# A feed-forward block computed as two-by-two block products: gate and up with seven products of block sums in place of eight

## What is computed

```python
D_FF = 2816
def rmsnorm(x, g):
    y = xf * lax.rsqrt(jnp.mean(xf * xf, axis=-1, keepdims=True) + EPS)
    return (y * g.astype(jnp.float32)).astype(x.dtype)
def swiglu(xn, w_gu, w_down):
    g, up = jnp.split(xn @ w_gu, 2, axis=-1)
    return (jax.nn.silu(g) * up) @ w_down
def trunk(...):
    for i in range(DEPTH):                       # DEPTH = 2
        ...                                      # norm, mixer, residual
        x = x + swiglu(rmsnorm(x, g_ffn[i]), f_w_gu[i], f_w_down[i])
    y = rmsnorm(x, g_final)
```

## Time and profile before

| | |
|---|---|
| profiled execution, its own time | 3015.9 us |
| its span from the first to the last instruction | 3014.1 us |
| median of three runs | 3014.09 us |
| PE busy / its weight loads | 2928.4 us (97%) / 2878.2 us (95%) |
| DVE busy | 1610.9 us (53%) |
| POOL busy | 1068.5 us (35%) |
| ACT busy | 408.6 us (14%) |
| mean granted TensorE clock | 0.989 |

### The profile page before, as it was taken

How to read it: one execution, slowest core, us unless ns; L and a number is a source line. 1 busy time by engine, 2 the same in 40 slices (tenths; PEclk the granted TensorE clock), 3 DMA queues, 4 the chain that set the end, 5 groups by cost and what they waited for, 6 DMA issues and landing times.

```text
span 3014.1 us, 41963 instructions
## 1 busy us (share of the span) xinstructions
PE 2928.4 (97%) x16670; PEld 2878.2 (95%) x16670; DVE 1610.9 (53%) x2328; ACT 408.6 (14%) x693; POOL 1068.5 (35%) x452
## 2 busy tenths in 40 slices
PE   6899999999999999999999999999999999999998
PEld 6899989899999999999899999999999999999998
DVE  6465564795555555555833465610655555555555
ACT  4112020230000000000311211200300000000004
POOL 4232223233333333333233223343433333333331
PEclk8999999999999999999999999999999999999999
DMA  2131121211111111111011121111111111111111
GB/s 92 43 70 39 49 44 42 51 36 42 42 42 41 37 40 42 42 42 42 28 43 42 32 68 42 36 42 42 43 42 42 42 42 42 42 42 42 42 42 63
DMA packets 198924, 133.76 MB, mean 44 GB/s; under 512 B 6731, under 2 KB 188619, under 8 KB 198860
## 3 DMA queue, kind: packets, MB, share of 16 engines
q1 hardware_dynamic: 198860, 132.87, 15.4%
HBM read 122.34 MB, written 10.51 MB: 44 GB/s over the span
## 4 chain that ended last, share of the span: by engine, by line
PE 89%; DVE 8%; issue 1%; POOL 1%; ACT 1%; DVEq 0%; POOLq 0%; ACTq 0%
PE ps L638 83%; DVE xn_lo L1353 2%; PE ps L1086 1%; DVE sq_f L1346 1%; POOL w_hi L594 1%; PE ps L1008 1%; PE ps L832 1%; PE ps L888 1%; PE ps L860 0%; PE ps L894 0%; PE ps L890 0%; PE ps L868 0%; PE ps L783 0%; DVE xT L1643 0%; DVE h_hi L1637 0%
## 5 line engine op out<-in xcount | busy, mean ns | idle before, releaser
L638 PE MATMUL ps<-xn_hi,w_hi 128*128 128x384 f32 x3480 | 1190.8, 342 | 16.7 <-DVE xT L1369 8.0
L594 POOL TENSOR_TENSOR w_hi<-w_raw,ones 128x1024 fp32r<-128x1024 f32 x213 | 535.1, 2512 | 1866.9 <-PE ps L638 1850.2
L638 PE MATMUL ps<-xn_lo,w_hi 128*128 128x384 f32 x3480 | 1178.5, 339 | 0.0
L638 PE MATMUL ps<-xn_hi,w_lo 128*128 128x384 f32 x3480 | 1178.2, 339 | 0.0
L638 PEld LDWEIGHTS ps<-xn_hi,w_hi 128*128 128x128 f32 x3480 | 657.6, 189 | 20.7 <-DVE xT L1369 8.2
L638 PEld LDWEIGHTS ps<-xn_lo,w_hi 128*128 128x128 f32 x3480 | 657.6, 189 | 1.5 <-issue 0.6
L638 PEld LDWEIGHTS ps<-xn_hi,w_lo 128*128 128x128 f32 x3480 | 656.9, 189 | 0.0
L598 POOL TENSOR_TENSOR w_lo<-w_raw,w_hi 128x1024 fp32r<-128x1024 f32 x213 | 528.7, 2482 | 16.7
L1685 DVE TENSOR_TENSOR xT<-xT,ps 128x384 f32<-128x384 f32 x528 | 279.5, 550 | 166.1 <-PE ps L638 166.0
L638 PE MATMUL ps<-hg_hi,w_hi 128*128 128x384 f32 x1056 | 358.5, 340 | 0.8 <-DVE xT L1685 0.8
L638 PE MATMUL ps<-hg_hi,w_lo 128*128 128x384 f32 x1056 | 356.5, 338 | 0.0
(11 more groups left out here) (262 smaller groups left out, 2342.3 us busy)
## 6 DMA issues: line engine op xcount, KB each, us to landing
w_raw<-in_f_w_gu_dram SPq DMA_DIRECT2D x88, 512.0 KB, 3.7
w_raw<-in_f_w_down_dram SPq DMA_DIRECT2D x44, 512.0 KB, 3.5
w_raw<-in_b_w_in_dram SPq DMA_DIRECT2D x32, 512.0 KB, 4.0
w_raw<-in_a_w_in_dram SPq DMA_DIRECT2D x24, 512.0 KB, 4.1
w_raw<-in_b_w_out_dram SPq DMA_DIRECT2D x16, 512.0 KB, 3.5
out_dram<-y_out SPq DMA_DIRECT2D x9, 512.0 KB
x_in<-in_x_prompt_dram SPq DMA_DIRECT2D x8, 512.0 KB, 5.7
c_nat<-in_state_C_dram SPq DMA_DIRECT2D x8, 512.0 KB, 5.9
```

Of the source, the lines that this page charges most:

```text
L594: nc.gpsimd.tensor_tensor(w_hi[s][:, :, :], w_raw[r][:, :, :], ones[:, :].unsqueeze(1).to_broadcast([P, KD, P]), ALU.mult)\
L638: ins = pe.matmul(out, w[slot][:, k, :], x(k), start=(first and n == 0), stop=(last_one and n == total - 1))
```

## The change

Gate and up are computed as products of two-by-two block matrices. For one of them, the two units c of 128 output features are the block rows, the two halves of the 1024 contraction features (KH = 4 blocks of 128 each) are the inner index, and two neighbouring quarters of the tokens (QT = 288 tokens) are the block columns; two such pairs s cover the 1152 tokens. Plain, a pair needs eight block products. The changed kernel makes seven (P1 to P7), each of a block or sum of blocks of the weights and a block or sum of blocks of the tokens, and gets the four results by adding products: P1+P2; (P1+P6+P5)+P7; P3+(P1+P6+P5); P4+(P1+P6+P7). One product is 4 contraction blocks x 3 passes = 12 matmuls of 288 columns.

- The sums of token blocks are made once for a layer, while its first iteration runs; they stand as seven blocks for each pair s (`xs_hi`, `xs_lo`). So the first iteration of a layer computes plainly, eight block products for a pair, also with 288 columns (`first_piece`), and ten iterations use the seven.
- The sums of weight blocks are made by POOL for every iteration, four of 128x512 for gate and four for up. Rounding weights (`round_left`) is now ACT's, the rest (`lower`) is POOL's, both in halves of 128x512. A weight half has one of 18 positions in an iteration: 0 to 6 gate, 7 to 13 up, 14 to 17 down; it takes the place of the one six positions ahead in the three slots, so it waits until PE has done with that.
- A product is added to its PSUM bank's neighbours by DVE: ACT copies P1 to SBUF (`keep_p1`, into the not yet used `hg_hi`), DVE adds P6, P5 and P7 in turn, then P2, P3 and P4. The gate result goes to SBUF (`hidden32`), Silu runs there in place, and ACT also rounds the hidden values (`hidden_hi`). All eight PSUM banks hold products now, in the down projection as well.
- The loads of the feed-forward weights wait for the rests of the halves that they overwrite, not for whole units.
- The down projection keeps its 144 matmuls of 384 columns.

```diff
 W_GATES = WeightPhase(None, 1, [0], [5])
 W_HEADS = WeightPhase(W_GATES, H, [2, 1, 0, 2, 0, 2, 1, 0], [3, 3, 3, 3, 2, 2, 5, 3])
...
+P1, P6, P5, P7, P2, P3, P4 = range(7)
+RIGHT = [X_B11, X_T2, X_T1, X_T3, X_B21, X_B22, X_T4]
+BANK_OF = [0, 1, 2, 3, 0, 2, 3]
+STEPS = [(P1, 0), (P1, 1), (P6, 0), (P6, 1), (P5, 0), (P5, 1), (P7, 0), (P7, 1),
+         (P2, 0), (P3, 0), (P4, 0), (P2, 1), (P3, 1), (P4, 1)]
...
+FINALS = [(0, 1), (1, 1), (0, 0), (0, 2), (0, 3), (1, 0), (1, 2), (1, 3)]
+FIRST_GATE = [(0, 0), (1, 0), (0, 1), (1, 1), (0, 2), (0, 3), (1, 2), (1, 3)]
+FIRST_UP = [(0, 1), (1, 1), (0, 3), (1, 3), (0, 0), (0, 2), (1, 0), (1, 2)]
+LAST_GROUP = [0, 1, 2, 2]
...
@@ -602,10 +742,59 @@
...
-            with pool.Fori(0, N_FFN) as i:
-                for u in range(6):
-                    split_unit(W_FFN0, i, u)
...
+                with pool.Fori(0, N_FFN - 1) as i:
+                    for kind in range(2):
+                        def low(j):
+                            lower(i, 7 * kind + j, left_source(j))
...
+                        low(P1)
...
+                        nc.gpsimd.tensor_tensor(left_sum[:, :, :], raw_half(1, 0), raw_half(1, 1), ALU.add)\
+                            .then_inc(left_summed, 1)
+                        pool.wait_ge(left_summed, so_far(1))
+                        nc.gpsimd.tensor_tensor(raw_half(1, 0), raw_half(1, 0), raw_half(0, 0), ALU.subtract)\
...
+                        nc.gpsimd.tensor_tensor(raw_half(0, 0), left_sum[:, :, :], raw_half(0, 0), ALU.subtract)\
+                            .then_inc(left_summed, 1)
+                        low(P6)
...
@@ -940,62 +1127,104 @@
...
+            def ffn(layer, n, bank_free):
...
+                def combine(out, pos, x, s, first, last_one, ready=None):
+                    for k in range(KH):
...
+                        for m, (w, r) in enumerate(((w_hi, xs_hi), (w_hi, xs_lo), (w_lo, xs_hi))):
+                            ins = pe.matmul(out, left(layer, w, pos)[:, k, :], r[:, s, x, k, :],
+                                            start=(first and k == 0 and m == 0),
...
+                        if g == 0:
+                            pe.wait_ge(hl, step(i, 8, 7 if first else 5))
+                        elif g == 1:
+                            pe.wait_ge(hl, step(i, 8, 8))
...
+                for c, q in FIRST_UP:
+                    pe.wait_ge(gs, FIRST_GATE.index((c, q)) + 1)
+                    first_piece(1, c, q)
+                down(0, True)
+                pe.wait_ge(x_los, 40 * (layer + 1))
+                with pe.Fori(0, N_FFN - 1) as i:
+                    for kind in range(2):
+                        for j, s in STEPS:
+                            if s == 0:
+                                pe.wait_ge(left_lo, prepared(layer, i, 7 * kind + j))
+                            o = BANK_OF[j]
+                            if j == P2:
+                                pe.wait_ge(p1_kept, product(layer, i, kind, s))
+                            elif j == P3:
+                                pe.wait_ge(p5_added, product(layer, i, kind, s))
+                            elif j == P4:
+                                pe.wait_ge(p7_added, product(layer, i, kind, s))
+                            elif kind == 0:
+                                pe.wait_ge(da, step(i, N_DOWN, 4 * s + o + 1))
+                            else:
+                                pe.wait_ge(gs, step(i, 8, finished(s, o)))
+                            combine(bank(4 * s + o, QT), 7 * kind + j, RIGHT[j], s, True, True)\
+                                .then_inc(prod_mm[j], 1)
+                    down(i, False)
...
@@ -1254,17 +1484,167 @@
...
-            def ffn(layer):
-                with act.Fori(0, N_FFN) as i:
-                    for c in range(2):
-                        for g in range(NG):
-                            act.wait_ge(g_scaled[layer], i * 6 + 3 * c + g + 1)
-                            act.activation(silu[:, c, g, :], bank(g), ACT.Silu).then_inc(g_silu[layer], 1)
...
+                def body(i, last_one):
+                    keep_p1(i, 0)
+                    round_sum(i, 0, P4, 6, prod_mm[P1], product(layer, i, 0, 1))
+                    for j in range(6):
+                        round_sum(i, 1, j, 7 + j, prod_mm[j + 1], product(layer, i, 0, 1))
+                    for at, (s, o) in enumerate(FINALS):
+                        act.wait_ge(g_scaled[layer], step(i, 8, at + 1))
+                        gated(i, s, o)
+                    keep_p1(i, 1)
+                    round_sum(i, 1, P4, 13, prod_mm[P1], product(layer, i, 1, 1))
+                    for pos in range(14, 17):
+                        round_down(i, pos, prod_mm[pos - 13], product(layer, i, 1, 1))
+                    for at, (s, o) in enumerate(FINALS):
+                        if at == 5:
+                            round_down(i, 17, prod_mm[P2], product(layer, i, 1, 1))
+                        hidden_hi(i, at, s, o)
+                    if not last_one:
+                        round_ahead(i)
...
@@ -1653,47 +2045,174 @@
...
+                for at, (c, q) in enumerate(FIRST_UP[4:], 4):
+                    hidden_lo(0, at - 1, FIRST_UP[at - 1][1] // 2, first_bank(*FIRST_UP[at - 1]) % 4)
+                    dve.wait_ge(first_mm, 16 * layer + 8 + at + 1)
+                    hidden(0, at, q // 2, first_bank(c, q) % 4)
+                hidden_lo(0, 7, FIRST_UP[7][1] // 2, first_bank(*FIRST_UP[7]) % 4)
...
+                        if kind == 1:
+                            for at, (s, o) in enumerate(FINALS):
+                                scale_silu(i, at, at, s, o)
+                        for s in range(2):
+                            dve.wait_ge(prod_mm[P6], product(layer, i, kind, s))
+                            dve.wait_ge(p1_kept, product(layer, i, kind, s))
+                            dve.tensor_tensor(piece_of(hg_hi32, s, 1), piece_of(hg_hi32, s, 0),
+                                              bank(4 * s + 1, QT), ALU.add)\
+                                .then_inc(p6_added, 1)
...
+                        for s in range(2):
+                            dve.wait_ge(prod_mm[P7], product(layer, i, kind, s))
+                            dve.wait_ge(p5_added, product(layer, i, kind, s))
+                            dve.tensor_tensor(piece_of(hg_hi32, s, 3), piece_of(hg_hi32, s, 1),
+                                              bank(4 * s + 3, QT), ALU.add)
+                            dve.tensor_tensor(bank(4 * s + 1, QT), piece_of(hg_hi32, s, 2),
+                                              bank(4 * s + 3, QT), ALU.add)\
+                                .then_inc(p7_added, 1)
+                            dve.wait_ge(p7_added, product(layer, i, kind, s))
+                            finish(s, s, 1)
...
+                            for n_, (j, o) in enumerate(((P2, 0), (P3, 2), (P4, 3))):
+                                at = 2 + 3 * s + n_
+                                dve.wait_ge(prod_mm[j], product(layer, i, kind, s))
+                                dve.tensor_tensor(bank(4 * s + o, QT), bank(4 * s + o, QT), piece_of(hg_hi32, s, o),
+                                                  ALU.add).then_inc(u_added, 1)
+                                dve.wait_ge(u_added, final_sum(layer, i, kind, s, n_))
+                                finish(at, s, o)
+                                if kind == 1 and at > 2:
+                                    hidden_lo(i, at - 1, *FINALS[at - 1])
+                    hidden_lo(i, 7, *FINALS[7])
```

More of the change, by code:

```diff
@@ L451, in _, with ffn @@
                 head(h)
-            def ffn(layer, phase):
+            def ffn(layer, before):
                 gu = f_w_gu[layer].rearrange("(k p) n -> p k n", p=P)
                 down = f_w_down[layer].rearrange("(k p) n -> k p n", p=P)
-                with sp.Fori(0, N_FFN) as i:
-                    for c in range(2):
-                        load(phase, i, 2 * c, gu[:, :, bass.ds(i * (2 * P) + c * P, P)])
-                        load(phase, i, 2 * c + 1, gu[:, :, bass.ds(i * (2 * P) + (D_FF + c * P), P)])
-                    for c in range(2):
-                        load(phase, i, 4 + c, down[bass.ds(i * 2 + c, 1)].rearrange("o p n -> (o p) n"))
@@ L463, in _, with load_gu, load_down @@
-            ffn(0, W_FFN0)
+                def load_gu(i, kind, c):
+                    sp.dma_start(w_raw[c][:, :, :], gu[:, :, bass.ds(step(i, 2 * P, kind * D_FF + c * P), P)])\
+                        .then_inc(f_loaded[c], 16)
+                def load_down(i, c):
+                    sp.dma_start(w_raw[c][:, :, :].rearrange("p k n -> p (k n)"),
+                                 down[bass.ds(step(i, 2, c), 1)].rearrange("o p n -> (o p) n")).then_inc(f_loaded[c], 16)
+                for c in range(2):
+                    sp.wait_ge(split, before.end - c)
+                    load_gu(0, 0, c)
@@ L616, in _ @@
                     split_unit(W_BO, i, u)
```

(9 more changed lines are left out.)

547 lines of the change are left out of this document (423 added, 124 removed).

## The result

The changed kernel took 2910.18 us (median of 4 runs, 2908.28 to 2916.6) against 3016.56 (3012.18 to 3020.6): a ratio of 0.9656, 95% interval 0.9638 to 0.9673. The forecast was 2931, range 2896 to 2992, so the time is inside it and 21 us under its middle. The profiled execution took 2909.89 with a span of 2908.2; before it was 3015.9 and 3014.1. So 106 us went where 83 were forecast.

A forecast was written before the change was run, and what follows sets the result against it. The loop was taken as bound by PE's matmul stream alone. 100.2 saved in the loops, less 3.0 for plain first iterations and 14 for layer starts, gives 83.2: 3015.9 to 2932.7, median 2931 us, range 2896 to 2992.

The forecast's parts named there:

- The stream, 135.6 ns: Gate and up in the loop: 336 matmuls of 288 columns at 135.6 ns, 5.01 us less an iteration, 100.2 in twenty.
- the three readings: Cost of a 288-column matmul: 135.6 ns (excess per instruction), 131.7 (per column) or 175.6 (weight load sets it).
- The down projection keeps its 25.3 us.: Down projection of each loop iteration: 144 matmuls at 175.6 ns, 25.3 us, unchanged.
- The other engines hide: Loop: POOL 32.5, ACT 19, DVE 40.2 us stay under PE's 70.9; fifth rest ready 0.8 us early; cost nothing.
- additions from PSUM are not held: DVE in the loop: the 28 additions of products, each with one PSUM input, do not contend with POOL.
- The layer starts, +14: Start of both layers' parts: waits and clock falls cost 8 us more in layer 1, 6 in layer 0; bounds 0 to 30.
- The 62 operations: DVE at layer 1's start, reciprocals to seventh rest: 62 x 0.45 + 4 x 1.3 = 33 us, so PE waits 5.5.
- T: Time zero for layer 1's start: the end of the mixer's matmuls; the seventh rest was put at T + 63.5.
- A: Rival for the matmul stream: excess belongs to the columns, 131.7 ns, 29 us less, 2902; chance 0.16.
- B: Rival: loop chain late at fifth rest or P5's addition; at 3 us an iteration 60 lost, 2991; chance 0.22.
- C: Rival: weight load sets the pace, 288 columns still cost 175.6 ns, 3231; decides above 146.7 ns; chance 0.09.
- D: Rival: starts of the layers' parts cost 30 or more, 2947 and up; mild form within the forecast's 0.50.

The follow-up runs named there:

- the second trace: The changed kernel run once more, unaltered, beside the two new start orders: 2907.20 us, ratio to before 0.9640.
- The run with eight banks: The kernel before with its down projection over eight PSUM banks in turn instead of six: 2996.27 us, ratio to before 0.9952.
- The new order: Changed kernel with ACT and DVE making token sums T4 behind the hidden values at each layer's start: 2894.13 us; with weight halves rounded earlier too, 2891.17.

## Why the prediction was right, and where it was off

- **The stream, 135.6 ns.** The choice among the three readings was right: an excess of the instruction, 14.4 ns in the loop against 15.6 put. The error was in the 15.6. It was a mean over two paces of the kernel before, 173.33 and 176.67, which I had seen as iterations of 75.1 and 76.4 and averaged. The changed loop has 134.4, and the term for gate and up measured 1010.9 - 903.4 = 107.5 us (20 iterations) instead of 100.2. Against the quick pace of before the products are worth 49.92 - 45.17 = 4.75 us an iteration at 134.4, and 49.92 - 44.80 = 5.12 at the 133.3 of the second trace's layer 0; 5.01 was put. Of the 107.5, 20 x 4.75 = 95 are the products and the other 12.5 are the 13 slow iterations of before, 0.96 us each.
- **"The down projection keeps its 25.3 us."** This step failed: it put the change of banks in the down projection at nothing. It fell to 24.96, and with the short waits that went the loops gave another 9.6 us. Of mixer B's 5.1 us 3.4 are two falls of the clock in the trace of before, as the rows above show. A wait of 90 ns, too small for the table of waits, had cost the kernel before some 18 us, most of them through the pace that it redrew. The run with eight banks shows it: it takes the 18 without any of the seven products. The changed kernel is 2996.3 - 2910.2 = 86 us faster than that one. That this is close to the 83 of the forecast is in part luck: between these two traces the loops give 94.1 (100.2 forecast), the starts take 14.7 (17.0 with the plain iterations), and mixer B gives 8.8, where the run with eight banks had three falls of the clock.
- **The other engines hide.** Right, and tight: the fifth rest is ready 0.65 us early (0.8 forecast) in all twenty iterations, by this row of DVE's timeline against the down projection's start at 967.49; it is held from 965.34 on while POOL works.

```profile
965.34 1.50 DVE L2088 TENSOR_TENSOR hg_lo<-hidden,hg_hi 128x288 fp32r<-128x288 f32 x1
```

```profile
965.24 1.29 POOL L751 TENSOR_TENSOR w_lo<-w_raw,w_hi 128x512 fp32r<-128x512 f32 x1 [5.16 <-ACT w_hi L1492]
```

  That additions from PSUM are not held was read right: the one at 1473.44 in the earlier trace rows ran beside this operation of POOL, the next behind that of the earlier trace rows.

```profile
1473.18 2.61 POOL L598 TENSOR_TENSOR w_lo<-w_raw,w_hi 128x1024 fp32r<-128x1024 f32 x1
```

- **The layer starts, +14.** The sum was right (with the plain iterations 17.0 forecast, 14.9 measured), its parts were not all. The waits: 3.8 for the weights (5.3 forecast), 5.3 and 6.5 at the first down projection (5.5); in layer 0 1.5 for the sum of squares and 1.0 for the first scaled gate, where 3 for token rests and 1.5 were put. The clock: two falls of 1.7 were put for layer 1, but a granted clock of 0.93 over 92.9 us is up to 6.5 us lost instead of 3.4 (up to, because PE waited anyway in a part of it). And the wait at the first down projection came out by luck. The 62 operations in its sum are a miscount: the list (8 + 8 + 24 + 7 + 7) has 54, which makes 29.5 us in place of 33, the seventh rest at T + 59.5 and a wait of 1.5, not 5.5. By its own list the forecast had no wait of that size. The trace has one because DVE was not busy to the end, as I had it: it idles there, behind ACT (DVE's timeline, then ACT's):

```profile
2110.79 7.37 DVE L2064 RECIPROCAL rstd_f<-rstd_f 128x384 f32<-128x384 f32 x3
...
2145.50 0.45 DVE L2083 TENSOR_TENSOR hidden<-hidden,ps 128x288 f32<-128x288 f32 x1
2148.89 0.46 DVE L2088 TENSOR_TENSOR hg_lo<-hidden,hg_hi 128x288 fp32r<-128x288 f32 x1 [2.94 <-ACT hg_hi L1525]
```

```profile
2145.25 3.27 ACT L1514 ACTIVATE xs_hi<-xs_lo 128x1152 fp32r<-128x1152 f32 x3 [0.55 <-DVE xs_lo L2112]
2148.43 0.42 ACT L1525 ACTIVATE hg_hi<-hidden 128x288 fp32r<-128x288 f32 x1
```

  ACT rounds token sums, which nobody needs before the second iteration, while the fifth hidden value waits behind them in its queue. From the reciprocals to the seventh rest DVE worked 29.7 us, as the 54 operations give, and idled for 4.5; eight operations too many in the count stood in for idle times that were not foreseen. The new order removes the wait of both layers.
- **The rivals.** A (excess by the column) gave 2902, nearer to the time than my forecast, and is wrong all the same: 512 columns take 227 ns, not the 231 of a column's share. What spoke for it, the 5 ns over 107 at 128 columns of float32, is no excess but the floor: float32r matmuls of 128 to 224 columns start the same 111.5 ns apart. B's mechanism is real at 0.65 us of slack and did not strike. C's floor exists at 111.5 ns, below the 146.7 from which it would have decided. D did not happen. The time was in the range, and 21 us under its middle, for the most part because of the slow pace and the short waits of before, which the forecast did not see.

## What to carry to other kernels

A float32r matmul with its own weight load cost its columns plus 12 to 17 ns here, down to a floor of 111.5 ns, so trading width for count is cheap above some 256 columns. The narrower matmuls took 1.3 us more an iteration, and a product saved was then worth its full time (48 matmuls, 6.45 us), as long as the other engines' chain ends ahead of PE. Look at the pace of the stream too, not only at its gaps: here equal iterations with different lengths were the sign that a short wait redraws it, and that wait was worth removing though it looks like nothing. Before a gain in an untouched stretch is explained, compare its granted clock in both traces. In a start-up phase put what the next matmul needs first in every engine's queue; when a late operation is explained by one engine's load, check whether that engine was idle.

## What the runs showed of the hardware that was not expected

- The spacing of equal matmuls at the same clock has discrete values that hold over tens of microseconds and through loop ends: 173.33 or 176.67 ns for 384 columns, 133.33 or 134.44 for 288. In the loops of before it changed only where PE had waited, if only for 90 ns. With a change of width it also changed without a wait, once, in the changed kernel's second trace (from 176.7 to 173.3 across a stretch of 288 columns). Without such a wait all twenty loop iterations of the kernel with eight banks had one length to 0.01 us. What sets the value is open.
- The floor of 111.5 ns a matmul with its own 128x128 load, from 224 columns down, though the load's record is 188 to 192 ns long.
- A wait of 2.2 us was followed by a fall of the clock in 8 of 20 iterations, each time for 3.4 us; around layer 1's start, with waits of 3.8 and 5.3 us, the granted clock was 0.93 over 92.9 us.
- Falls of 3.4 us also come inside the untouched mixer B, in some executions and not in others: two in the first trace of before, three in that with eight banks, none in the first of the changed kernel and two in its second.
